# Loading a paged key/value cache: single pages from two queues, or gathers of 128 blocks from Pool

## The chip, the cores and the metric

The kernel runs on one core of a Trainium2 chip. The metric is the time of one execution on the device in microseconds. The engines have the names that the profile gives them: PE (TensorE, matmuls; PEld are its weight loads), DVE (VectorE), ACT (ScalarE), POOL (GpSimd) and SP (SyncE, which here only issues DMAs). SPq, POOLq and so on are the sequencers of these engines.

## What is computed

One step of a hybrid decoder layer: a prompt of 1024 tokens (causal attention over itself) and 8 sequences of 4 new tokens each, whose attention runs over 8192 cached tokens per sequence. The cache is paged. For the change only this part of the reference matters:

```python
k_past = cache_k[l, page_table].reshape(bs, past, N_HEADS, 2, QK_HEAD)
v_past = cache_v[l, page_table].reshape(bs, past, N_HEADS, V_HEAD)
k_all = jnp.concatenate([k_past.astype(k.dtype), k], axis=1)
v_all = jnp.concatenate([v_past.astype(v.dtype), v], axis=1)
o = diff_attend(q, q_pos_s, k_all, v_all, k_pos_s, lam)
```

`page_table` has 8 x 64 page numbers. A page holds 128 tokens; a token's keys (and its values) are 4 heads x 128 numbers of 4 bytes, so 2 KB, and a page is 256 KB of keys and 256 KB of values. All of it together is 512 pages x 2 x 256 KB, some 268 MB. Every cached token is visible to every query, so the order in which the tokens of a page lie in SBUF changes nothing, as long as keys and values have the same one.

## The kernel before, in words

The kernel has five stages, each closed by `stage_end`, where PE, ACT, DVE and SP wait for each other: (1) modulation, (2) the input projection, (3) attention, (4) output projection and the first half of the feed-forward, (5) the down projection. The change lies in stage 3, which in the trace runs from about 423 to 1287 us. The prompt's attention and the samples' attention are woven into each other there.

The samples are taken one after the other: `step(b, ...)` for b = 0 to 7. A step has REVS = 4 rounds r of RING = 4 groups g; a group is GP = 4 pages, so 1 MB of keys and 1 MB of values. `k_ring` and `v_ring` have four slots of one group each. In step b, for each group, DVE turns the keys (`turn_keys`, L1432, 32x32 blocks, `k_ring` to `k_turned`, and the slot is free when that is done: `k_free`), PE multiplies them with the queries (`key_group`, L852), and then PE multiplies the values of sample b-1 with the probabilities of sample b-1 (`value_group`, L862; the slot is free after it: `v_free`). So keys of b and values of b-1 are used side by side. In between lie the prompt's pieces (`scores` L818, `turn_rows` L825, `weigh_rows` L832, `maxima`, `combine`, `take_rows`): one tile of 128 prompt rows in each round, and the tiles differ in size (1, 2, 5, 6 or 0, 3, 4, 7 as multiples of 128 columns, plus one). Between two steps stands `softmax(b)`: scores of the sample to probabilities, turned by PE and copied to `p_t` (L424). It is a chain over PE, DVE and ACT in which no ring slot is used. After step 7 there are 16 value groups alone. PE and ACT run two steps in each turn of a loop, from step 1 on.

The pages are loaded by `load_pages` (L442 to L463), which runs on SP for the groups 0 and 2 and on Pool for the groups 1 and 3. For each page it reads the page's number from SBUF into a register (`value_load`), and before a group's first page it waits for the slot. Each page is a DMA of its own (L449) of 128 rows of 2 KB, token p to partition p. Its counts on `k_in[g]` and `v_in[g]` rise by 64 a group. In each queue the keys of b+1 and the values of b stand in turn. Pool issues one more transfer ahead of its pages: `v_rows` (L631, 2 MB, the prompt's values), after `conv_s_in`. DVE begins the stage with a memset (L1369) and a little work on `conv_s`. SP begins it with `page_row` (L552) and six small transfers.

Of the kernel before, what the change touches and what calls it, by code (L numbers as in the profile page):

```python
# [30 lines left out]
I32 = mybir.dt.int32  # L31
ALU = mybir.AluOpType
ACT = mybir.ActivationFunctionType
AX_X = mybir.AxisListType.X
ds = bass.ds

P = 128
QUAD = 32
# [31 lines left out]
def constants(z):  # L70

    p = np.arange(P)
    out = {}
    out["ident"] = np.eye(P)

    out["quad_fold"] = (p[:, None] % QUAD == np.arange(QUAD)[None, :])

    h, q = p // QUAD, p % 8
# [26 lines left out]
    where, n = {}, 0  # L105
# [6 lines left out]
def build(nc, z, io, const_at, n_const):  # L112
    T, D, B, S, H, HD, F = z.T, z.D, z.B, z.S, z.H, z.HD, z.F
    KC, NT, CH, NCH, NF, BS, AW, CC = z.KC, z.NT, z.CH, z.NCH, z.NF, z.BS, z.AW, z.CC
# [4 lines left out]
    GP, RING = 4, 4  # L119
    REVS = z.PAGES // (GP * RING)  # L120
    NEW0 = z.PAGES * QUAD
    SC = NEW0 + QUAD
# [5 lines left out]
    with ExitStack() as ctx:  # L128
# [27 lines left out]
        def sem(name):  # L156
            return ctx.enter_context(nc.semaphore(name))
# [56 lines left out]
        s_quads = ar("s_quads", [P, 2, WB])  # L214
        dense_end = max(ar.at, stage0 + 4 * ((2 * RING + 2) * GP * AW + B * z.PAGES + NT * AW + SC + 2 * T + P + 64))
        ar.at = dense_end
# [17 lines left out]
        ar.at += 2 * GP * AW * 4 - 7 * CC * 4  # L234
        page_row = ar("page_row", [1, B * z.PAGES], mybir.dt.int32)
        v_rows = ar("v_rows", [P, NT, AW])
# [56 lines left out]
        v_out = io["new_v_prompt"].rearrange("l b t h d -> (l b t) (h d)")  # L293
        k_pages = io["cache_k"].rearrange("l n p h d -> (l n) p (h d)")
        v_pages = io["cache_v"].rearrange("l n p h d -> (l n) p (h d)")
        x_dram = io["x_prompt"].rearrange("b t d -> (b t) d")
# [45 lines left out]
        v_in = [sem(f"v_in{g}") for g in range(RING)]  # L342
        pages_in = sem("pages_in")
        k_free, v_free, scored, s_bank_free = sem("k_free"), sem("v_free"), sem("scored"), sem("s_bank_free")
# [94 lines left out]

        def load_pages(eng, par):  # L440


            def group(pages, ring, landed, free, b, r, g):
                for j in range(GP):
                    page = eng.value_load(page_row[0:1, ds((b * REVS + r) * (RING * GP) + (g * GP + j), 1)],  # L445
                                          min_val=0, max_val=z.POOL - 1)
                    if j == 0:
                        eng.wait_ge(free, (b * REVS + r) * RING + g + 1)
                    eng.dma_start(ring[:, g, j, :], pages[ds(page, 1)].rearrange("o p d -> p (o d)")  # L449
                                  ).then_inc(landed[g], 16)  # L450

            keys, values = (k_pages, k_ring, k_in, k_free), (v_pages, v_ring, v_in, v_free)
            with eng.Fori(0, REVS) as r:
                for g in range(par, RING, 2):
                    group(*keys, 0, r, g)
            with eng.Fori(0, B - 1) as b:
                with eng.Fori(0, REVS) as r:
                    for g in range(par, RING, 2):
                        group(*keys, b + 1, r, g)
                        group(*values, b, r, g)  # L460
            with eng.Fori(0, REVS) as r:
                for g in range(par, RING, 2):
                    group(*values, B - 1, r, g)  # L463

# [6 lines left out]
        def _(sp):  # L471
# [79 lines left out]

            sp.dma_start(page_row[:], io["page_table"].rearrange("b n -> (b n)").rearrange("(o n) -> o n", o=1)).then_inc(pages_in, 16)  # L552
            for j in range(3):
                sp.dma_start(conv_s[:, j, :], u_ext[:, j:j + S, :]).then_inc(conv_s_in, 16)
            for j in range(3):
                sp.dma_start(conv_s[:, 4 + j, :], io["conv_w"][0, j].partition_broadcast(QUAD)).then_inc(conv_s_in, 16)
            sp.wait_ge(pages_in, 16)
            load_pages(sp, 0)
            stage_end(sp, 3)
# [68 lines left out]
        def _(pool):  # L628
# [3 lines left out]

            pool.wait_ge(pages_in, 16)
            load_pages(pool, 1)


# [27 lines left out]
        def _(pe):  # L664
# [192 lines left out]
            def value_group(b, r, g, stop):  # L857

                pe.wait_ge(v_in[g], (b * REVS + r + 1) * (16 * GP))
                for j in range(GP):  # L860
                    for h in range(H):
                        last = mm(psum[QUAD * h:QUAD * (h + 1), 2, 0:P], p_t[:, (r * RING + g) * GP + j, :],  # L862
                                  v_ring[:, g, j, h * HD:(h + 1) * HD], start=False, stop=stop and j == GP - 1)
                last.then_inc(v_free, 1)
# [362 lines left out]
        def _(dve):  # L1227
# [139 lines left out]
            dve.sem_inc(o_free, 1)  # L1367
            dve.sem_inc(scored, 2)
            link(v.memset(q_zero[:], 0.0))  # L1369
            dve.wait_ge(conv_s_in, 96)  # L1370
# [57 lines left out]
            def turn_keys(b, r, g):  # L1428
                n = (b * REVS + r) * RING + g
                dve.wait_ge(k_in[g], (b * REVS + r + 1) * (16 * GP))  # L1430
                dve.wait_ge(scored, n + 1)
                v.transpose(k_turned[:, g % 2].rearrange("p j n -> p (j n)"), k_ring[:, g].rearrange("p j n -> p (j n)")  # L1432
                            ).then_inc(k_free, 1)
# [267 lines left out]
```

## Time and profile before

| | us |
|---|---|
| median of 3 runs | 2371.07 (2368.57 to 2372.17) |
| the profiled execution, its own time | 2369.3 |
| its span in the trace | 2367.6 |
| granted clock of PE, mean share of 2.4 GHz | 0.88 |
| stage 3 in the trace | about 423 to 1287 |

The span is cut into 40 slices of 59.2 us in the page's second part; stage 3 fills about the 8th to the 22nd of them. A digit there is the busy share in tenths. A row of the timeline begins with start and duration in us; the square brackets at its end say how long the engine had been idle before it and what ended that. In the row of a window, "DMA share" is the mean busy share of the 16 DMA engines. It can be over 1, since the packets of an engine overlap.

### The profile page before, as it was taken

To read this page: it belongs to the slowest core of one execution; us is meant where nothing else is said; L and a number is where in the kernel's file an instruction comes from. 1 tells how busy PE (TensorE), PEld (TensorE's weight loads), DVE (VectorE), ACT (ScalarE), POOL (GpSimd) and SP (SyncE) were. 2 spreads that over 40 slices of the span, in tenths; PEclk is the share of its full clock that TensorE was granted. 3 is DMA by queue.
4 is the path that set the end of the run, shared out by engine and by line. 5 is a ranking of instruction groups with operands and counts; after the bars stand their busy time and mean duration, and the time that the engine had idled before them with its cause. 6 is when DMAs were issued, how large, how long until landed. Compare 5 with 4: busy or idle time off the path is not lost.

```text
span 2367.6 us, 47877 instructions
## 1 busy us (share of the span) xinstructions
PE 1879.2 (79%) x17492; PEld 1497.8 (63%) x17492; DVE 1058.0 (45%) x1528; ACT 488.9 (21%) x831; POOL 354.9 (15%) x544
## 2 busy tenths in 40 slices
PE   5699999567565765766665894999999997999992
PEld 1378899345444554544544893777777776888881
DVE  2424221666675675666661567121112112455457
ACT  0300111021212112121220204111211111333331
POOL 0000000223242432334332106100000000000003
PEclk7799999578887877878886897999999998999996
DMA  9611222789898989989888210121212123311112
GB/s 311 250 36 35 72 71 101 255 259 334 295 386 289 386 300 327 337 290 386 315 310 285 107 46 8 55 70 55 86 55 69 56 86 139 128 41 37 37 32 91
DMA packets 210968, 404.21 MB, mean 171 GB/s; under 512 B 24426, under 2 KB 88938, under 8 KB 210788
## 3 DMA queue, kind: packets, MB, share of 16 engines
q1 hardware_dynamic: 161012, 261.51, 31.9%
q0 software_dynamic: 41488, 136.35, 15.6%
q10 hardware_dynamic: 8320, 4.19, 0.6%
q8 instruction: 116, 1.90, 0.3%
q14 instruction: 32, 0.26, 0.0%
HBM read 377.53 MB, written 24.51 MB: 170 GB/s over the span
## 4 chain that ended last, share of the span: by engine, by line
PE 60%; SPq 13%; DVE 10%; DMA 9%; issue 6%; ACT 1%; DVEq 0%; ACTq 0%
PE psum L753 26%; PE psum L1002 11%; PE psum L761 10%; SPq L445 7%; SPq L449 6%; DMA v_ring<-cache_v 4%; DMA ada_w<-w_ada 3%; DVE k_turned L1432 2%; PE psum L1009 2%; DVE p_t L424 2%; PE psum L736 2%; PE psum L862 1%; DVE x_lo L1282 1%; DMA k_ring<-cache_k 1%; PE psum L852 1%
## 5 line engine op out<-in xcount | busy, mean ns | idle before, releaser
L1432 DVE STREAM_TRANSPOSE k_turned<-k_ring 128x2048 f32<-128x2048 f32 x128 | 295.4, 2308 | 12.6 <-DMA k_ring<-cache_k 12.3
L753 PE MATMUL psum<-x_hi,w_hi 128*128 128x512 f32 x896 | 281.3, 395 | 0.0
L852 PE MATMUL psum<-k_turned,q_blocks 128*32 128x128 f32 x4096 | 171.2, 319 | 136.2 <-DVE k_turned L1432 136.1
L753 PE MATMUL psum<-x_lo,w_hi 128*128 128x512 f32 x896 | 277.2, 391 | 0.0
L753 PE MATMUL psum<-x_hi,w_lo 128*128 128x512 f32 x896 | 276.1, 389 | 0.0
L852 PEld LDWEIGHTS psum<-k_turned,q_blocks 128*32 128x32 f32 x4096 | 127.9, 128 | 194.8 <-issue 148.2
L1301 DVE TENSOR_TENSOR w_lo<-w_raw,w_hi 128x2048 fp32r<-128x2048 f32 x37 | 86.9, 2350 | 361.9 <-ACT w_hi L1057 352.2
L862 PE MATMUL psum<-v_ring,p_t 128*32 128x128 f32 x4096 | 173.9, 325 | 65.1 <-DMA v_ring<-cache_v 65.0
L1002 PE MATMUL psum<-d_hi,h_hi 128*128 128x256 f32 x704 | 209.2, 297 | 12.1 <-DVE d_lo L1646 11.0
L1002 PE MATMUL psum<-d_lo,h_hi 128*128 128x256 f32 x704 | 199.9, 284 | 0.0
L1002 PE MATMUL psum<-d_hi,h_lo 128*128 128x256 f32 x704 | 199.7, 284 | 0.0
L753 PEld LDWEIGHTS psum<-x_hi,w_hi 128*128 128x128 f32 x896 | 165.7, 188 | 44.9 <-ACT h_out L1193 4.5
L449 POOL DMA_DIRECT2D k_ring<-cache_k x256 | 139.0, 543 | 363.5 <-issue 182.4
L862 PEld LDWEIGHTS psum<-v_ring,p_t 128*32 128x32 f32 x4096 | 140.0, 132 | 83.5 <-DMA v_ring<-cache_v 79.1
L753 PEld LDWEIGHTS psum<-x_lo,w_hi 128*128 128x128 f32 x896 | 168.8, 188 | 35.7
L753 PEld LDWEIGHTS psum<-x_hi,w_lo 128*128 128x128 f32 x896 | 168.5, 188 | 35.9
L761 PE MATMUL psum<-w_hi,x_hi 128*128 128x256 f32 x640 | 182.9, 286 | 0.0
L761 PE MATMUL psum<-w_lo,x_hi 128*128 128x256 f32 x640 | 181.8, 284 | 0.0
L761 PE MATMUL psum<-w_hi,x_lo 128*128 128x256 f32 x640 | 181.8, 284 | 0.0
L1645 DVE TENSOR_TENSOR h_lo<-h_all,h_hi 128x1024 fp32r<-128x1024 f32 x88 | 107.6, 1223 | 145.6 <-ACT d_hi L1218 145.6
L449 POOL DMA_DIRECT2D v_ring<-cache_v x256 | 138.5, 541 | 208.5 <-issue 175.2
L1002 PEld LDWEIGHTS psum<-d_hi,h_hi 128*128 128x128 f32 x704 | 135.1, 192 | 48.1 <-issue 44.4
(228 smaller groups left out, 2562.0 us busy)
## 6 DMA issues: line engine op xcount, KB each, us to landing
k_ring<-cache_k SPq DMA_DIRECT2D x256, 256.0 KB, 8.1
k_ring<-cache_k POOLq DMA_DIRECT2D x256, 256.0 KB, 6.1
v_ring<-cache_v SPq DMA_DIRECT2D x256, 256.0 KB, 8.9
v_ring<-cache_v POOLq DMA_DIRECT2D x256, 256.0 KB, 6.1
ada_w<-w_ada SPq DMA_DIRECT2D x12, 2048.0 KB, 9.2
w_raw<-w_in SPq DMA_DIRECT2D x12, 1024.0 KB, 5.2
w_raw<-w_gate SPq DMA_DIRECT2D x11, 1024.0 KB, 5.3
w_raw<-w_up SPq DMA_DIRECT2D x11, 1024.0 KB, 6.2
```

The source lines that it names most:

```text
L424: last = copy(to[QUAD * a:QUAD * (a + 1), :, j], got[:, :, :, a, :])
L445: page = eng.value_load(page_row[0:1, ds((b * REVS + r) * (RING * GP) + (g * GP + j), 1)], min_val=0, max_val=z.POOL - 1)
L449: eng.dma_start(ring[:, g, j, :], pages[ds(page, 1)].rearrange("o p d -> p (o d)")).then_inc(landed[g], 16)
L736: last = mm(psum[q:q + QUAD, 4 + s, 0:WB], x_t_s[:, k, :], w_raw[:, s, k, :], start=k < 4, stop=k >= KC - 4)
L753: last = mm(psum[:, 2 * ft + c, 0:CH], w[:, s, k, ft * P:(ft + 1) * P], x[:, k, c * CH:(c + 1) * CH], start=k == 0 and j == 0, stop=k == K ...
L761: last = mm(psum[:, t % TB, 0:WB], x[:, k, t * P:(t + 1) * P], w[:, s, k, :], start=k == 0 and j == 0, stop=k == KC - 1 and j == 2)
L852: last = mm(psum[QUAD * h:QUAD * (h + 1), g % 2, 0:GP * QUAD], q_blocks[:, h, d, :], k_turned[:, g % 2, :, h * HD + d * QUAD:h * HD + (d + ...
L862: last = mm(psum[QUAD * h:QUAD * (h + 1), 2, 0:P], p_t[:, (r * RING + g) * GP + j, :], v_ring[:, g, j, h * HD:(h + 1) * HD], start=False, ...
L1002: last = mm(psum[:, down_bank(par, pair), (t % 2) * WB:(t % 2 + 1) * WB], x[:, s, t * P:(t + 1) * P], w[:, s, :], start=k == 0 and j == 0 ...
L1301: v.tensor_tensor(w_lo[:, s], w_raw[:, s], w_hi[:, s], ALU.subtract).then_inc(w_lo_done, 1)
L1432: v.transpose(k_turned[:, g % 2].rearrange("p j n -> p (j n)"), k_ring[:, g].rearrange("p j n -> p (j n)")).then_inc(k_free, 1)
L1645: v.tensor_tensor(h_lo[:, s, :], h_all[:, k, :], h_hi[:, s, :], ALU.subtract)
```

## The change

The pages come in gathers. A page is seen as 32 blocks of 8 KB (four tokens each), and one indirect DMA brings 128 blocks, which is a group of four pages: partition 32 j + a gets block a of the group's page j. The numbers of the blocks stand in `page_idx`, one column for each group. DVE makes it in four instructions, one for each j, from `page_all`, which is the page table spread over all partitions: 32 x page + lane, where lane is a new constant. All gathers, 128 of keys and 128 of values, are issued by Pool, written out without loops and without register loads; SP issues no pages any more. Each group now counts 16 on its semaphore. What PE, ACT and DVE do with the rings stays the same.

```diff
+    out["lane"] = (p % QUAD)[:, None]
...
-        page_row = ar("page_row", [1, B * z.PAGES], mybir.dt.int32)
+        page_all = ar("page_all", [P, B * z.PAGES], I32)
+        page_idx = ar("page_idx", [P, B * z.PAGES // GP], mybir.dt.uint32)
...
-        k_pages = io["cache_k"].rearrange("l n p h d -> (l n) p (h d)")
-        v_pages = io["cache_v"].rearrange("l n p h d -> (l n) p (h d)")
+        k_pages = io["cache_k"].rearrange("l n (p s) h d -> (l n p) (s h d)", p=QUAD)
+        v_pages = io["cache_v"].rearrange("l n (p s) h d -> (l n p) (s h d)", p=QUAD)
...
-        def load_pages(eng, par):
...
+        def load_pages(pool):
+            def gather(rows, ring, landed, free, b, r, g):
+                n = (b * REVS + r) * RING + g
+                pool.wait_ge(free, n + 1)
+                pool.indirect_dma_start(ring[:, g].rearrange("p s d -> p (s d)"), None, rows,
+                                        bass.IndirectOffsetOnAxis(page_idx[:, n:n + 1], 0)).then_inc(landed[g], 16)
+            for b in range(B + 1):
+                for r in range(REVS):
+                    for g in range(RING):
+                        if b < B:
+                            gather(k_pages, k_ring, k_in, k_free, b, r, g)
+                        if b:
+                            gather(v_pages, v_ring, v_in, v_free, b - 1, r, g)
...
-            sp.dma_start(page_row[:], io["page_table"].rearrange("b n -> (b n)").rearrange("(o n) -> o n", o=1)).then_inc(pages_in, 16)
+            sp.dma_start(page_all[:], io["page_table"].rearrange("b n -> (b n)").partition_broadcast(P)).then_inc(pages_in, 16)
...
-            sp.wait_ge(pages_in, 16)
-            load_pages(sp, 0)
             stage_end(sp, 3)
...
-            pool.wait_ge(pages_in, 16)
-            load_pages(pool, 1)
+            pool.wait_ge(page_idx_ready, GP)
+            load_pages(pool)
...
-                pe.wait_ge(v_in[g], (b * REVS + r + 1) * (16 * GP))
+                pe.wait_ge(v_in[g], (b * REVS + r + 1) * 16)
...
+            dve.wait_ge(pages_in, 16)
+            for j in range(GP):
+                r = slice(QUAD * j, QUAD * (j + 1))
+                v.tensor_scalar(page_idx[r, :], page_all[r, :].rearrange("p (n j) -> p n j", j=GP)[:, :, j], float(QUAD), C("lane")[r],
+                                ALU.mult, ALU.add).then_inc(page_idx_ready, 1)
             link(v.memset(q_zero[:], 0.0))
...
-                dve.wait_ge(k_in[g], (b * REVS + r + 1) * (16 * GP))
+                dve.wait_ge(k_in[g], (b * REVS + r + 1) * 16)
```

## Rows read from the trace of the kernel before

**Rows 1.** The page's second part: busy tenths and GB/s in 40 slices.
```profile
DVE  2424221666675675666661567121112112455457
DMA  9611222789898989989888210121212123311112
GB/s 311 250 36 35 72 71 101 255 259 334 295 386 289 386 300 327 337 290 386 315 310 285 107 46 8 55 70 55 86 55 69 56 86 139 128 41 37 37 32 91
```
**Rows 2.** The page's fourth part: the chain that ended last, by engine.
```profile
PE 60%; SPq 13%; DVE 10%; DMA 9%; issue 6%; ACT 1%; DVEq 0%; ACTq 0%
```
**Rows 3.** Windows: stretch, length, busy us of each engine, PE clock, DMA share, GB/s.
```profile
742.00:750.00 8.00, 6.89 (x130) 5.35 (x130) 6.00 (x9) 1.47 (x6) 1.62 (x3) 0.63 0.56 171
760.00:830.00 70.00, 50.65 (x863) 38.44 (x864) 43.58 (x56) 14.03 (x38) 28.89 (x53) 0.83 1.04 386
834.00:844.00 10.00, 2.04 (x42) 1.25 (x42) 8.62 (x21) 2.02 (x4) 0.00 (x0) 0.50 0.08 31
1250.00:1284.00 34.00, 18.91 (x352) 14.25 (x352) 0.00 (x0) 0.00 (x0) 11.65 (x22) 0.65 0.98 349
```
**Rows 4.** Timeline of DVE: first or last keys turned, steps 0, 1, 3, 4, 6, 7.
```profile
442.05 2.31 DVE L1432 STREAM_TRANSPOSE k_turned<-k_ring 128x2048 f32<-128x2048 f32 x1 [0.62 <-DMA k_ring<-cache_k]
511.58 2.30 DVE L1432 STREAM_TRANSPOSE k_turned<-k_ring 128x2048 f32<-128x2048 f32 x1
534.28 2.31 DVE L1432 STREAM_TRANSPOSE k_turned<-k_ring 128x2048 f32<-128x2048 f32 x1
740.30 2.31 DVE L1432 STREAM_TRANSPOSE k_turned<-k_ring 128x2048 f32<-128x2048 f32 x1
813.75 2.30 DVE L1432 STREAM_TRANSPOSE k_turned<-k_ring 128x2048 f32<-128x2048 f32 x1
841.96 2.31 DVE L1432 STREAM_TRANSPOSE k_turned<-k_ring 128x2048 f32<-128x2048 f32 x1
1126.26 2.30 DVE L1432 STREAM_TRANSPOSE k_turned<-k_ring 128x2048 f32<-128x2048 f32 x1
1149.01 2.30 DVE L1432 STREAM_TRANSPOSE k_turned<-k_ring 128x2048 f32<-128x2048 f32 x1
```
**Rows 5.** Waits: engine and line, what for, us in total, times, longest.
```profile
PEld psum L862 <- DMA v_ring<-cache_v: 79.1, 45, 6.3
PE psum L862 <- DMA v_ring<-cache_v: 65.0, 40, 6.0
```
**Rows 6.** Timeline: page issues of SP (four in a row) and of Pool.
```profile
742.79 3.83 SPq L449 DMA_DIRECT2D k_ring<-cache_k  x4
747.65 4.68 SPq L449 DMA_DIRECT2D v_ring<-cache_v  x4
818.28 3.85 SPq L449 DMA_DIRECT2D v_ring<-cache_v  x4
...
746.36 0.54 POOL L449 DMA_DIRECT2D k_ring<-cache_k  x1 [21.92 <-DVE k_turned L1432]
747.59 0.54 POOL L449 DMA_DIRECT2D k_ring<-cache_k  x1 [0.69 <-issue]
```
**Rows 7.** Timeline: Pool's 2 MB issue, and one page issue beside DVE's L1393.
```profile
429.73 1.07 POOL L631 DMA_DIRECT2D v_rows<-new_v_prompt  x1 [429.12 <-DMA conv_s<-conv_w]
...
811.91 0.86 POOL L449 DMA_DIRECT2D k_ring<-cache_k  x1 [0.69 <-issue]
811.96 0.69 DVE L1393 TENSOR_SCALAR a_rows<-e_rows,soft 128x896 f32<-128x896 f32 x1
```
**Rows 8.** Timeline and window in stage 4: a 4 MB load in rows of 4 KB.
```profile
1312.22 0.37 SPq L566 DMA_DIRECT2D x<-x_prompt  x1
...
1316.00:1324.00 8.00, 8.00 (x54) 6.78 (x55) 0.00 (x0) 0.00 (x0) 0.00 (x0) 0.66 1.02 415
```
**Rows 9.** Timeline of PE: first and last value groups after step 7.
```profile
1243.26 5.18 PE L862 MATMUL psum<-v_ring,p_t 128*32 128x128 f32 x128
...
1282.38 3.73 PE L862 MATMUL psum<-v_ring,p_t 128*32 128x128 f32 x64 [1.60 <-DMA v_ring<-cache_v]
```
**Rows 10.** Timeline: SP's table load and DVE's work at the start of stage 3.
```profile
423.73 0.25 SPq L552 DMA_DIRECT2D page_row<-page_table  x1
...
425.14 1.76 DVE L1369 MEMSET q_zero<- 128x2048 f32 x1 [9.18 <-issue]
429.17 2.11 DVE L1372 TENSOR_TENSOR conv_s<-conv_s 32x512 f32<-32x512 f32 x3 [2.26 <-DMA conv_s<-conv_w]
```

More of the change, by code:

```diff
@@ L214, in build @@
         s_quads = ar("s_quads", [P, 2, WB])
-        dense_end = max(ar.at, stage0 + 4 * ((2 * RING + 2) * GP * AW + B * z.PAGES + NT * AW + SC + 2 * T + P + 64))
+        dense_end = max(ar.at, stage0 + 4 * ((2 * RING + 2) * GP * AW + B * z.PAGES + B * z.PAGES // GP + NT * AW + SC + 2 * T + P + 64))
         ar.at = dense_end
@@ L342, in build @@
         v_in = [sem(f"v_in{g}") for g in range(RING)]
-        pages_in = sem("pages_in")
+        pages_in, page_idx_ready = sem("pages_in"), sem("page_idx_ready")
         k_free, v_free, scored, s_bank_free = sem("k_free"), sem("v_free"), sem("scored"), sem("s_bank_free")
@@ L437, in build @@
         block = ctx.enter_context(nc.Block())
-        def load_pages(eng, par):
[L443 to L463, printed above, removed]
+        def load_pages(pool):
[11 more added lines that the diff above has]
+                            gather(v_pages, v_ring, v_in, v_free, b - 1, r, g)
         def fetch_head(eng, h):
```

## The prediction

> **What bounds the kernel now.** I looked first at the slices of the page. Stage 3, some 864 of 2368 us, is the only long stretch in which the DMA engines stand at 8 or 9 tenths, while DVE stands at 5 to 7 there [rows 1]. The chain that ended last gives 60% to PE (mostly the projections outside stage 3), and 22% to SP's sequencer and DMA together [rows 2], and these two are what the change touches. The windows say what that is: inside a step the DMA engines are full, share 1.04, and move 386 GB/s, while PE is busy 50.65 and DVE 43.58 of 70 us [rows 3]. Between two steps they stand nearly still, 31 GB/s, since all eight ring slots are full and the softmax chain uses none. So a step is paced partly by the transfer, and the softmax between steps by its own chain. That consumption waits for data is seen in the waits: PE's value groups waited 79.1 us (weight loads) and 65.0 us (matmuls) for `v_ring`; the two overlap, so it is some 80 us, not 144 [rows 5].
>
> The period of a step is (1149.01 - 534.28) / 6 = 102.5 us [rows 4]. It moves 32 groups of 1.049 MB, 33.6 MB, which at 386 GB/s is 86.9 us. Some 15 us of DMA time per step are lost, partly in the stand-still, partly in the ramp after it: in the first 8 us of a step the engines moved only 171 GB/s [rows 3], because SP needs 4.9 us to issue the four pages of a group (742.79 to 747.65) and Pool 1.22 us for each page (746.36 to 747.59) [rows 6].
>
> **Part 1: who issues, and at what cost.** Now SP and Pool each issue half. SP needs 75.5 us for 15 groups (742.79 to 818.28), 5.0 us each, without a stop for a slot [rows 6]. Both together can thus issue a group in about 2.5 us, and the DMA engines take 1.049 / 0.386 = 2.72 us for it. After the change Pool alone must issue one gather per group. If it costs less than about 2.5 us, it is hidden behind the transfer; if it costs more, Pool becomes the bound. No row shows an indirect DMA. The near rows: Pool's issue of 128 rows of 2 KB is 0.54 us [rows 6], and that of 1024 such rows is 1.07 us [rows 7], so rows cost Pool almost nothing in a plain issue (0.53 us for 896 more). From below, then, a gather costs 0.54 us. From above I take a gather as four page issues with their register loads, 4 x 1.22 = 4.9 us, as if each quarter's table had to be read by itself. The value I take is 1.2 to 2 us, near one page issue with one look into SBUF, because the instruction names 128 blocks and no page issue's fixed part should be paid four times. It is hidden. Both ends stay in the rivals.
>
> Break-even. If Pool stands still for the 28 us between steps (813.75 to 841.96 is 28.2 us, 1126.26 to 1149.01 is 22.7 us, from the last keys turned to the first [rows 4]) it must issue 24 gathers in the rest: (102.5 - 28 - 5) / 24 = 2.9 us. If it uses that time for the eight refills, 102.5 / 32 = 3.2 us. Above about 3 us per gather the kernel gets slower.
>
> **Part 2: the transfer.** Pages come in rows of 2 KB now, blocks of 8 KB later. Nothing here moves 8 KB rows, but a load in rows of 4 KB ran at 415 GB/s over 8 us with a DMA share of 1.02 [rows 8], against 386 for the pages [rows 3]. So a group takes between 2.72 us (nothing gained) and 2.53 us (415 GB/s); I take 2.55. Below 386 I see no reason from rows, except for a gather that is spread unevenly over the 16 engines; that goes with the slow rival. Over the 24 groups that must arrive inside a step this is 65.2 us before and 61.2 after, 4 us less per step.
>
> **Part 3: order and ramp.** SP and Pool drift apart: by 818.28 SP has issued its last group of the step's cycle [rows 6] while Pool still lags some 7 us, so keys of the next sample go ahead of values that PE waits for now. One queue keeps the order of use. Also the first free slot is refilled by one instruction and not over 4.9 us. Both take the ramp of about 5 us and part of the V waits away. The floor is then the consumption by itself: step 0, without any value stream, needs 511.58 - 442.05 = 69.5 us from the first to the last keys turned, about 3 of it waits for the first loads, and step 3 needs 73.5 us [rows 4]. The mean over the steps 1 to 7 (112 such transposes, of which the first and last of step 3 stand there) is 74.4. I take 70 for each: 4.4 x 7 = 31 us. The bound from the other side is the same pace as now, 0, and at best 66, which is 59 us. The stretch between two steps is 102.5 - 74.4 = 28 us on average and 22.7 at its shortest (after step 6), and a part of the difference is the last value group landing late. Another part is the turning point of PE's loop and the head's work, and stays. Of 6 x 5.4 = 32 us I take 10.
>
> **Part 4: the end.** After step 7 sixteen value groups run alone. The first four come from full slots (1243.26), the last ends at 1286.1 [rows 9]. Twelve groups took from 1244.6 (the first of the four done) to 1286.1, 3.46 us each, at 349 GB/s with the DMA share below 1 [rows 3], since a slot is refilled page by page, four times 1.22 us. A single gather needs its issue and the transfer, 12 x 2.6 to 2.9 + 3 for the first landing: 34 to 38 us instead of 41.5. I take 6 us less.
>
> **Part 5: the start.** DVE now waits for the table before its memset and has four small instructions more (32 partitions x 128 numbers, about 0.3 us each by the L1372 rows' 0.7 us for 512). The table was issued at 423.73 and the memset began at 425.14; after it DVE stood idle 2.26 us [rows 10]. So 2 to 3 us more meet 2.3 us of cover: 0 to 1 us. SP's table load is 256 KB now and not 2 KB, ahead of the six small ones, less than 1 us at 386 GB/s. Pool's wait for `page_idx` stands behind `conv_s_in`, which comes later (429.73 [rows 7]); behind it are all gathers, and DVE's first keys wait for them. Before, SP began pages beside Pool's `v_rows`; now 2 MB of `v_rows` stand ahead of the first keys in the one queue. Step 0 waited for its keys 0.62 us at 442.05 [rows 4]; 3.1 MB at 386 GB/s are 8.1 us from 431, about 440. I take 0, with 3 us either way. SP is free and only reaches the stage's end earlier: nothing. That keys and values of one queue wait for each other in turn (behind a wait for `v_free` stand the next keys) costs nothing as long as the ring is four deep: the order of waiting is that of use.
>
> **Sum.** 31 + 10 + 6 + 0 = 47 us off the profiled execution's 2369.3 us, 2322. It lay 1.8 us below the median of the runs, so 2324 us. The ends of the terms: 0 + 0 + 3 - 3 = 0 us with nothing hidden gained, and 59 + 20 + 8 + 3 = 90 us at best, 2281.
>
> **A rule against it.** One page issue beside DVE's L1393 took Pool 0.86 us and not 0.54 [rows 7]. The Trainium skill (SBUF — State Buffer, "SBUF: two separate sides") says that a DMA issued from GpSimd can't get its descriptors written while DVE runs an operation in a two-port mode, and that DMAs from SP are free of this; the change moves half of the pages from SP to Pool. That row would agree, with 0.3 us.
>
> **The rivals.** (A) Pool is the bound: a gather costs more than about 3 us because each of the 128 block numbers is worked on by itself. For it: no row shows one, and the plain rows cover a regular pattern only. Against it: 1024 rows in 1.07 us. At 3.5 us the period is 32 x 3.5 = 112 us, 9.5 more, 67 for seven steps and 1 at the end: 2371 + 68 = 2439 us. At 4.9 us it is 157 us, and some 2770. It decides from 3.0 us on. (B) The pages land sooner, but nobody needs them sooner: DVE and PE pace the step as they do in step 0 with its small waits. Then only the end and a third of Part 3 remain, 6 + 12 = 18 us: 2353. For it speaks the irregular pace of the transposes with the ring full. (C) Pool's issues are held up by DVE. At most the time of L1393, 0.69 us in the row, in each of the 28 rounds of seven steps falls on the path: 19 us of the 47 are lost, 2343. (D) The gathers gain what the lost second queue costs (two queues side by side kept each DMA engine fed): about 2371.
>
> **How the numbers follow.** Forecast, 2285 to 2340: 0.50. (A) slower, from about 2376 up: 0.24, half of it above 2430. (B) and (C), 2340 to 2366: 0.17. (D), within 0.2%, 2366 to 2376: 0.08. Better than 2285: 0.01. A difference of 0.2%, 4.7 us, is about what a measurement of this kernel can tell from none. Faster 0.68, same 0.08, slower 0.24. The range of 8 in 10 goes from 2288 to 2430 and leaves out about 0.02 below and 0.12 to 0.15 above. The likeliest case's own range is 2285 to 2340.
>
> **What would show it.** In the profile after: gathers on Pool with a mean duration below 2.5 us, and Pool idle before them mostly for `k_turned` or `v_ring`; in a step's middle 400 GB/s and more; the DMA slices of stage 3 no higher than now, but fewer; PE's waits for `v_ring` far below 79.1 us; the period of a step near 96 us; the value groups at the end 3 us apart. The prediction is wrong if Pool is back to back in its gathers and the GB/s of a step's middle fall below 386, which is (A), or if the waits for `v_ring` vanish and the period stays above 100 us, which is (B).

## The result, and the profile after

The changed kernel takes 2299.79 us in the median of 4 runs (2296.46 to 2304.27), the kernel before 2370.01 us beside it. The ratio is 0.9704 (95% interval 0.9685 to 0.9723): 70 us or 3.0% faster, where 2324 us was predicted, in a range of 2288 to 2430. The profiled execution took 2304.27 us, 65.0 us less than the profiled one of before.

The page of the changed kernel: the DMA engines and the chain.

```profile
DVE  2324121577776685776734564111121112465547
DMA  9701132677898988989975110121212214311102
GB/s 312 265 30 43 37 109 92 232 288 300 334 410 321 418 330 327 414 330 396 363 311 224 37 37 19 55 91 55 73 55 69 77 55 173 106 42 38 37 28 94
...
PE 65%; DVE 17%; DMA 11%; issue 5%; ACT 1%; DVEq 0%; POOL 0%; SPq 0%; ACTq 0%
...
L448 POOL DMA_INDIRECT k_ring<-cache_k,page_idx x128 | 120.6, 943 | 330.8 <-DVE k_turned L1429 322.0
L448 POOL DMA_INDIRECT v_ring<-cache_v,page_idx x128 | 120.7, 943 | 207.3 <-PE psum L854 199.9
```

A gather costs Pool 0.943 us, and Pool is idle before it because a ring slot is not free yet (322.0 and 199.9 us of waiting). SP's sequencer, 13% of the chain before [rows 2], is gone from it, and DVE rose from 10 to 17%. Slices of stage 3 now reach 418 GB/s where they reached 389 [rows 1].

Windows in the middle of steps 1, 3 and 4 of the changed kernel (columns as in rows 3), and the waits of PE and its weight loads for `v_ring`:

```profile
560.00:580.00 20.00, 13.60 (x311) 10.28 (x299) 16.52 (x19) 4.49 (x11) 8.43 (x9) 1.00 1.01 417
740.00:760.00 20.00, 13.47 (x336) 10.43 (x336) 16.32 (x22) 3.94 (x12) 8.55 (x10) 1.00 1.01 418
840.00:860.00 20.00, 15.09 (x304) 12.01 (x308) 15.79 (x22) 3.32 (x9) 8.02 (x9) 0.89 1.01 419
...
PEld psum L854 <- DMA v_ring<-cache_v,page_idx: 17.7, 12, 3.1
PE psum L854 <- DMA v_ring<-cache_v,page_idx: 13.3, 12, 2.8
```

The rate rose from 386 [rows 3] to 417 to 419 GB/s with the engines full in both cases, and the waits for values fell from 79.1 and 65.0 us [rows 5] to 17.7 and 13.3. The twelve that are left are those after step 7. The first and last keys turned of steps 0, 1, 3, 4 and 7:

```profile
443.95 2.30 DVE L1429 STREAM_TRANSPOSE k_turned<-k_ring 128x2048 f32<-128x2048 f32 x1
507.67 2.30 DVE L1429 STREAM_TRANSPOSE k_turned<-k_ring 128x2048 f32<-128x2048 f32 x1
531.70 2.31 DVE L1429 STREAM_TRANSPOSE k_turned<-k_ring 128x2048 f32<-128x2048 f32 x1
721.16 2.31 DVE L1429 STREAM_TRANSPOSE k_turned<-k_ring 128x2048 f32<-128x2048 f32 x1
788.18 2.31 DVE L1429 STREAM_TRANSPOSE k_turned<-k_ring 128x2048 f32<-128x2048 f32 x1 [0.47 <-DMA k_ring<-cache_k,page_idx]
814.36 2.31 DVE L1429 STREAM_TRANSPOSE k_turned<-k_ring 128x2048 f32<-128x2048 f32 x1
1094.07 2.30 DVE L1429 STREAM_TRANSPOSE k_turned<-k_ring 128x2048 f32<-128x2048 f32 x1
```

Step 3 went from 73.5 us [rows 4] to 67.0, the period of a step from 102.5 to (1094.07 - 531.70) / 6 = 93.7. Taken over all steps (128 transposes in each trace), the 65 us are made up like this, in us:

| part of stage 3 | before | after | difference |
|---|---|---|---|
| up to the first keys turned (442.05, 443.95) | | | +1.9 |
| step 0, first to last keys turned | 69.5 | 63.7 | -5.8 |
| steps 1 to 7, mean | 74.3 | 67.1 | 7 x -7.25 = -50.8 |
| between steps 0 and 1 | 22.7 | 24.0 | +1.3 |
| between the others, mean | 28.0 | 26.7 | 6 x -1.28 = -7.7 |
| last keys turned to the last value group's end | 63.4 | 59.5 | -3.9 |
| sum | | | -65.0 |

Behind the last value group 1081.5 us of the span were left before and 1081.3 are now. All of the gain lies in stage 3, and four fifths of it inside the steps with both streams. Only that line of the table is steady. A second profiled execution of the changed kernel (the run `after_again` below) has 67.1 us for the steps 1 to 7 too, but 66.8 for step 0, 26.1 for the mean stretch between steps and 61.6 for the end.

In the steps 1 to 7 of before PE waited 48.3 us for values (32 times) and DVE 9.6 us for keys (11 times). In the changed kernel there is no such wait for values, and 5.1 us for keys are left. That is 52.8 us less, about the 50.8 of the table. The clock of PE moved as well. The sums of the seven steps, from the first to the last keys turned, before and after:

```profile
sum 520.40, PE 356.56 PEld 262.45 DVE 367.75 ACT 82.50 POOL 198.31; mean PE 50.94 PEld 37.49 DVE 52.54 ACT 11.79 POOL 28.33
sum 469.64, PE 331.93 PEld 252.92 DVE 367.87 ACT 82.65 POOL 187.83; mean PE 47.42 PEld 36.13 DVE 52.55 ACT 11.81 POOL 26.83
```

DVE is busy for as long as before, PE for 3.5 us less a step, at a granted clock of 0.82 to 0.87 before and 0.88 to 0.94 after (1.0 is 2.4 GHz, 0.5 is 1.2 GHz). How much of the gain comes through the clock, and whether it rose because PE waited less, no run separates.

### The profile page after: what moved, and what is told of

Same layout as the page of the kernel before. It is cut to its first block, busy times and chain, and to the rows that moved or that the text cites. A ratio compares the mean times of both kernels' runs of the same rounds, so it can differ in the third digit from the quotient of the medians.

```text
span 2302.5 us, 40476 instructions
## 1 busy us (share of the span) xinstructions
PE 1839.8 (80%) x17492; PEld 1481.2 (64%) x17492; DVE 1056.6 (46%) x1532; ACT 489.0 (21%) x831; POOL 319.1 (14%) x287
## 4 chain that ended last, share of the span: by engine, by line
PE 65%; DVE 17%; DMA 11%; issue 5%; ACT 1%; DVEq 0%; POOL 0%; SPq 0%; ACTq 0%
PE psum L745 27%; PE psum L994 12%; PE psum L753 10%; DVE k_turned L1429 6%; DMA k_ring<-cache_k,page_idx 6%; DMA ada_w<-w_ada 3%; PE psum L844 2%; PE psum L854 2%; PE psum L1001 2%; DVE p_t L426 2%; PE psum L728 2%; PE psum L824 1%; DVE x_lo L1274 1%; DMA v_ring<-cache_v,page_idx 1%; DVE soft L1380 1%
## 5 line engine op out<-in xcount | busy, mean ns | idle before, releaser
L844 PE MATMUL psum<-k_turned,q_blocks 128*32 128x128 f32 x4096 | 157.0, 300 | 151.0 <-DVE k_turned L1429 150.7
L844 PEld LDWEIGHTS psum<-k_turned,q_blocks 128*32 128x32 f32 x4096 | 117.0, 119 | 204.6 <-issue 152.9
L854 PE MATMUL psum<-v_ring,p_t 128*32 128x128 f32 x4096 | 163.9, 307 | 17.6 <-DMA v_ring<-cache_v,page_idx 13.3
L448 POOL DMA_INDIRECT k_ring<-cache_k,page_idx x128 | 120.6, 943 | 330.8 <-DVE k_turned L1429 322.0
L994 PEld LDWEIGHTS psum<-d_hi,h_hi 128*128 128x128 f32 x704 | 135.0, 192 | 48.3 <-issue 44.1
L854 PEld LDWEIGHTS psum<-v_ring,p_t 128*32 128x32 f32 x4096 | 136.4, 125 | 25.3 <-DMA v_ring<-cache_v,page_idx 17.7
L448 POOL DMA_INDIRECT v_ring<-cache_v,page_idx x128 | 120.7, 943 | 207.3 <-PE psum L854 199.9
```

The lines of the kernel that those rows point to most:

```text
L448: pool.indirect_dma_start(ring[:, g].rearrange("p s d -> p (s d)"), None, rows, bass.IndirectOffsetOnAxis(page_idx[:, n:n + 1], 0)).then_i ...
L844: last = mm(psum[QUAD * h:QUAD * (h + 1), g % 2, 0:GP * QUAD], q_blocks[:, h, d, :], k_turned[:, g % 2, :, h * HD + d * QUAD:h * HD + (d + ...
L994: last = mm(psum[:, down_bank(par, pair), (t % 2) * WB:(t % 2 + 1) * WB], x[:, s, t * P:(t + 1) * P], w[:, s, :], start=k == 0 and j == 0 ...
```

## The experiments

Three causes were in question, all of them touched by the change: the size of the rows in which pages come (2 or 8 KB), the order in which two queues or one bring the groups, and the price of the issue (eight register loads and DMAs for a pair of groups, or two instructions). The kernel before was timed beside each of them, and ratios (with their 95% interval) are against it. Not all kernels ran on the same chip, so the ratio is the better measure where two of them are compared. The diffs show the line that matters; the views of the cache, counts and waits that change with it are left out.

**Plain DMAs of 1 MB from Pool.** In `load_pages` of the changed kernel:

```diff
-                pool.indirect_dma_start(ring[:, g].rearrange("p s d -> p (s d)"), None, rows,
-                                        bass.IndirectOffsetOnAxis(page_idx[:, n:n + 1], 0)).then_inc(landed[g], 16)
+                pool.dma_start(ring[:, g], rows[n * GP:(n + 1) * GP].rearrange("j p d -> p j d")).then_inc(landed[g], 16)
```

> The changed kernel, but each gather is a plain DMA from Pool of four neighbouring pages (1 MB), in rows of 2 KB, token p of each page to partition p. It leaves the page table out of account: pages are read in their order in the pool. One queue, one instruction a group and the order of use are as in the changed kernel; only the rows are those of before. Theory R (the gain is the rate of 8 KB blocks against 2 KB rows): the middle of a step stays at 386 GB/s, the steps from first to last keys turned stay at 71 to 74 us, time 2340 to 2365 us. Theory I (the gain is one cheap issue in the order of use, and the row size is no matter): 2295 to 2310 us with steps of 67 us.

2337.15 us, ratio 0.9863 (0.9841 to 0.9885). That is in the range of neither theory, 3 us below that of R. Theory R was right on what it said of the rate, 384 GB/s, and of the steps:

```profile
560.00:580.00 20.00, 12.30 (x278) 9.23 (x282) 14.66 (x20) 3.43 (x9) 6.02 (x8) 1.00 1.02 384
```

The steps 1 to 7 take 71.1 us on average, and late in a step keys are turned 5.4 us apart with a wait for `k_ring` before them (the last two of step 3 stand here). That is two groups at 386 GB/s, 2 x 2.72, so here the transfer sets the pace:

```profile
797.81 2.31 DVE L1428 STREAM_TRANSPOSE k_turned<-k_ring 128x2048 f32<-128x2048 f32 x1 [0.79 <-DMA k_ring<-cache_k]
803.23 2.31 DVE L1428 STREAM_TRANSPOSE k_turned<-k_ring 128x2048 f32<-128x2048 f32 x1 [0.89 <-DMA k_ring<-cache_k]
```

But the time is 31 us below before with the same rows and the same rate. So not quite half of the gain had to be looked for in the issue or the order.

**The same in blocks of 8 KB, from Pool.**

```diff
+                pool.dma_start(ring[:, g].rearrange("p s d -> p (s d)"), rows[n * P:(n + 1) * P]).then_inc(landed[g], 16)
```

> As the kernel with plain DMAs of 1 MB from Pool, but in blocks of 8 KB, 128 neighbouring blocks to the 128 partitions. It leaves the page table out of account too. Against the changed kernel only the indirection is gone. Both theories: 2295 to 2305 us, as the changed kernel, 415 to 420 GB/s in the middle of a step; the issue on Pool 0.5 us and not 0.94. If the gather's own cost or its spread over the DMA engines matters, this one is faster by more than 5 us.

2296.22 us, ratio 0.9691 (0.9672 to 0.9710), 417 to 418 GB/s, steps of 66.4 us, with 0.55 us for an issue on Pool where the gather takes 0.943. It is 41 us faster than its twin with 2 KB rows on the same chip. The indirection of the real kernel costs nothing that these runs can tell: 0.9704 and, in a later comparison, 0.9689.

**Both from SP.** The call of `load_pages` moves from Pool to SP, behind the wait for the table; nothing else.

> The plain DMAs of 1 MB in rows of 2 KB, issued by SP and not by Pool (the page table is left out of account, as there). Theory R: as from Pool, 2340 to 2365 us, 377 to 390 GB/s. Theory I: 2295 to 2310 us. If DMAs from Pool suffer from DVE, this one is faster than its twin from Pool by more than 5 us.

> The plain DMAs of 1 MB in blocks of 8 KB, issued by SP (the page table is left out of account). Both theories: 2295 to 2305 us. If DMAs from Pool suffer from DVE: 2285 to 2295 us.

2328.11 us (0.9827, 0.9809 to 0.9845) with 2 KB and 2293.48 us (0.9681, 0.9664 to 0.9698) with 8 KB. Against Pool they are 9 and 3 us faster. The first pair's intervals only just touch, the second's overlap. The 9 us are more than the 5 us that the expectation named as the sign of DVE holding up Pool's DMAs. But Pool's issues of the values have 751 ns as shortest and as median and 760 as longest, so DVE did not hold those issues up. In windows of 20 us the 2 KB kernel from SP shows 376 to 385 GB/s and that from Pool 361 to 384; inside the steps both reach 386. Of the 9 us 4.5 lie in the steps 1 to 7 (70.4 us each and not 71.1). What they are stays open.

**Smaller blocks, more gathers.** The table gets two or four columns for a group, and `gather` issues as many instructions, each of 128 blocks of 4 KB or of 2 KB:

```diff
+                for m in range(2):
+                    pool.indirect_dma_start(ring[:, g, 2 * m:2 * (m + 1)].rearrange("p s d -> p (s d)"), None, rows,
+                                            bass.IndirectOffsetOnAxis(page_idx[:, 2 * n + m:2 * n + m + 1], 0)).then_inc(landed[g], 16)
```

> The changed kernel with two gathers a group, each of 128 blocks of 4 KB (two pages), and a table twice as wide, made by two DVE instructions. A gather takes Pool 0.94 us, with 0.30 us between two in a row: 2.5 us a group, just under the transfer's 2.5 to 2.6 us. Rival A of the prediction puts the break-even near 3 us a group: so still faster than before, 2300 to 2325 us. The rate in the middle of a step is 400 to 415 GB/s, by the 4 KB load in stage 4.

> The changed kernel with four gathers a group, each of one page in 128 rows of 2 KB. Pool needs 4 x 1.24 = 5.0 us a group: Pool is the bound. By rival A's formula the period of a step is 32 x 5.0 = 159 us, 65 more than in the changed kernel, times seven, and the steps 0 and 8 move 16 groups each at 5.0 us: 2300 + 457 + 40 = about 2800 us. If a gather's cost goes with its bytes and not with its blocks, it is far less, below 2400 us.

Two gathers: 2316.98 us, ratio 0.9782 (0.9763 to 0.9801), steps of 68.9 us. Four: 2812.68 us (a single execution), within 13 us of what rival A's formula gave. Both windows, first of two and then of four gathers a group, and Pool in the latter:

```profile
740.00:760.00 20.00, 13.12 (x282) 10.05 (x285) 15.81 (x21) 2.69 (x9) 15.12 (x17) 0.91 1.03 409
```
```profile
740.00:760.00 20.00, 11.11 (x141) 8.57 (x142) 6.27 (x7) 1.11 (x3) 15.13 (x17) 0.50 0.70 210
...
763.63 0.95 POOL L448 DMA_INDIRECT k_ring<-cache_k,page_idx  x1 [0.30 <-issue]
764.88 0.95 POOL L448 DMA_INDIRECT k_ring<-cache_k,page_idx  x1 [0.30 <-issue]
```

Pool is back to back at 1.25 us a gather, 5.0 us a group, and 1.049 MB / 5.0 us are the 210 GB/s. A gather's price does not go with its bytes. All gathers here have 128 block numbers, so no run tells a price for each number from a price for the instruction. With two, Pool needs 2.5 us a group and the transfer 2.56 at 409 GB/s; that is below the break-even of about 3 us and still faster than before. It also gives the third point for the rate: rows of 2 KB 384 to 386, blocks of 4 KB 407 to 409, of 8 KB 415 to 420 GB/s, with the DMA engines full each time.

**Blocks of 8 KB in the kernel before.** Page j of a group goes to the partitions 32 j to 32 j + 31, everything else as before:

```diff
-                    eng.dma_start(ring[:, g, j, :], pages[ds(page, 1)].rearrange("o p d -> p (o d)")
+                    eng.dma_start(ring[QUAD * j:QUAD * (j + 1), g].rearrange("p s d -> p (s d)"), pages[ds(page, 1)].rearrange("o p d -> p (o d)")
```

> The kernel before (SP and Pool, one DMA for each page with register loads), but a page goes as 32 blocks of 8 KB to 32 partitions and not as 128 rows of 2 KB to 128 partitions. Theory R: some of the gain comes although the issue stays as it was, 2325 to 2345 us. Theory I: 2360 to 2375 us. A third possibility is that 32 partitions are served by fewer DMA engines at a time, and the kernel gets slower than 2371 us.

2703.86 us (five executions, 2670.54 to 2716.00), ratio 1.1443 (1.1411 to 1.1474): neither of the two theories, but the third possibility, as far as the direction goes. The engines are not fewer, however:

```profile
740.00:760.00 20.00, 9.76 (x171) 7.52 (x160) 6.32 (x6) 1.22 (x3) 4.49 (x9) 0.68 1.02 238
```

The share is 1.02, so the engines are full on average, and they move 238 GB/s (220 to 273 in other stretches of the stage). The Trainium skill (SBUF — State Buffer, "Door 1: The DMA port swizzle") says that 32 neighbouring partitions, and also the first 64, reach only eight of SBUF's sixteen ports for DMA. That fits this row; no run here tells it from another limit on 32 partitions. The size of the DMA is not what makes it slow, since before moved the same 256 KB at a time over 128 partitions at 386 GB/s. Of the forms tried here, the gather alone brings scattered pages in blocks of 8 KB over all 128 partitions.

**Order or price of the issue.** The plain DMAs of 1 MB in 2 KB rows, but SP issues the groups 0 and 2 and Pool 1 and 3 (`for g in range(par, RING, 2)`), as in the kernel before:

> The plain DMAs of 1 MB in rows of 2 KB (page table left out of account), but issued as before by two queues: SP the groups 0 and 2, Pool 1 and 3. Against the kernels with one queue only the order across the queues is as before; against the kernel before only the issue is cheap (one instruction a group, no register loads). Part 3 of the prediction put the drift of the two queues against each other beside the slow issue as a cause. If the drift counts: 2345 to 2365 us. If only the price and delay of the issue count: 2325 to 2340 us, as with one queue.

2372.31 us, ratio 0.9998 (0.9983 to 1.0013), 7 us above the range for the drift. That is the time of the kernel before, although each group costs one instruction and no register load. Against one queue from Pool the second queue costs 35 us, or 32 by the ratios. The rate is the same; this window and these rows are of step 3:

```profile
760.00:820.00 60.00, 38.44 (x758) 28.26 (x758) 41.36 (x49) 10.35 (x26) 7.48 (x10) 0.86 1.03 386
...
PEld psum L855 <- DMA v_ring<-cache_v: 67.9, 30, 4.8
...
754.15 0.37 SPq L448 DMA_DIRECT2D v_ring<-cache_v  x1
...
773.49 1.93 PE L855 MATMUL psum<-v_ring,p_t 128*32 128x128 f32 x31 [3.98 <-DMA v_ring<-cache_v]
```

SP's issue at 754.15 is the sixth group of the step (743.87, 747.23, 747.67, 751.28 and 752.03 come before it in the two queues). Six groups at 386 GB/s are 16.3 us, so in the order of issue it would have been there about 762. By the trace it landed 19.3 us after its issue, at 773.4, and PE waited 3.98 us for it. Pool's issue of 757.84, made later, took 12.6 us and had landed at 770.4. With two queues later groups move at the same time as the one that is needed first, and can land before it. The queues do not share the engines evenly either. The view of the DMA queues from 760 to 780 us (packets, MB, share of the engines; then issues with the us from issue to landing):

```profile
q0 software_dynamic: 1275, 4.95, 64.3%
q1 hardware_dynamic: 1377, 2.73, 37.8%
...
v_ring<-cache_v SPq DMA_DIRECT2D x2, 1024.0 KB, 21.5
v_ring<-cache_v POOLq DMA_DIRECT2D x2, 1024.0 KB, 10.4
```

q0 is Pool's queue and q1 is SP's. Both move about as many packets, but Pool's hold 3.9 KB on average and SP's 2.0, so SP's groups take twice as long to land. In the kernel with one queue PE's waits of the steps are gone: 20.3 us in 12 waits are left, the twelve after step 7. DVE's waits for keys rose in turn, from 13.4 us (15 times) to 34.6 (39 times).

The equal times of this kernel and of before do not show that the price of the issue is worth nothing. The parts differ: step 0 takes 63.3 us here and not 69.5, and the steps 1 to 7 take 75.7 and not 74.3. In before Pool needs 1.22 us for each page, and its queue and SP's move about the same there, 13.70 and 13.18 MB from 760 to 830 us. The cheap issue lifted that limit, and Pool's queue went ahead of SP's. What the issue alone is worth in two queues with 2 KB rows stays open.

**Two queues with 8 KB.**

> The plain DMAs of 1 MB in blocks of 8 KB (page table left out of account), issued by two queues, SP the groups 0 and 2, Pool 1 and 3. With rows of 2 KB the second queue cost 35 us (2372 against 2337). If queue and block size are independent causes: 2296 + 35, so 2325 to 2335 us, with the steps near 71 us and 415 GB/s. If the faster blocks make the order of landing harmless, since the transfer no longer paces the step: 2295 to 2310 us.

2300.64 us, ratio 0.9713 (0.9688 to 0.9737), steps of 66.4 us:

```profile
740.00:760.00 20.00, 13.85 (x338) 10.73 (x337) 16.39 (x21) 4.27 (x12) 2.65 (x5) 1.00 1.01 416
...
PEld psum L855 <- DMA v_ring<-cache_v: 27.0, 20, 5.5
```

The causes don't add up: with 8 KB blocks the second queue costs nothing that can be told from the one-queue ratio of 0.9691. The view of the queues (760 to 780 us) shows one difference, beside the higher rate:

```profile
q0 software_dynamic: 570, 4.16, 50.8%
q1 hardware_dynamic: 568, 4.15, 50.0%
...
v_ring<-cache_v SPq DMA_DIRECT2D x2, 1024.0 KB, 18.3
v_ring<-cache_v POOLq DMA_DIRECT2D x2, 1024.0 KB, 18.1
```

Both queues have packets of 7.3 KB on average (small ones counted in) and move the same, and their groups land after the same time. Which of the two, the even share or the transfer that no longer sets the pace, makes the second queue harmless, no run separates.

| plain DMAs of 1 MB | rows of 2 KB | blocks of 8 KB |
|---|---|---|
| two queues | 0.9998 | 0.9713 |
| one queue (Pool) | 0.9863 | 0.9691 |

Alone, the block size brings 2.9% and the single queue 1.4% (1.7% when SP issues it); together they bring 3.1%.

**A version that is faster.** From step 7 on the key ring has nothing to hold, and the twelve waits that are left are for values. The last sample's groups 4 to 7 and 12 to 15 are loaded into `k_ring` (and read there by `value_group`), and DVE's memset stands ahead of its wait for the table. In the first form the eight gathers of the groups 8 to 15 went alternately to `k_ring` and `v_ring`, in the second the four for `v_ring` go first:

```diff
+                        if b == B:
+                            last = RING + (B - 1) * REVS * RING + g + 1
+                            if r == 0:
+                                gather(v_pages, k_ring, k_in, k_free, B - 1, 1, g, RING + (B * REVS - 1) * RING + g + 1)
+                                gather(v_pages, v_ring, v_in, v_free, B - 1, 0, g, last - RING)
+                            elif r == 2:
+                                gather(v_pages, v_ring, v_in, v_free, B - 1, 2, g, last)
+                            elif r == 3:
+                                gather(v_pages, k_ring, k_in, v_free, B - 1, 3, g, last + RING)
+                            continue
```

> The changed kernel with two edits: the values of the last sample also go into the key ring, which is free then (second and fourth round), so that four more groups are there when the last softmax ends; and the memset of q_zero stands ahead of DVE's wait for the table. The first takes 4 x 2.5 = 10 us from the end of the stage, the second 1 to 2 us from its start: 2286 to 2290 us. If the DMA engines are not idle after step 7, or the start waits for the keys anyway: 2295 us.

> The version with the last sample's values in both rings, with the order of the last eight gathers put right: the four that go into the value ring come first, as they are used first and their slots are free first (from about 1180 us on and not from 1185). The eight need 20 us and 3 for the landing: the last value group ends near 1206 us and not at 1215.9, so 2281 to 2286 us, and 14 us or more below the changed kernel beside it. If the order was not the fault of its forerunner: 2292 us again.

> The changed kernel once more, as the measure for its neighbours on the same chip: 2297 to 2303 us.

The first form took 2292.61 us (0.9675, 0.9657 to 0.9693), while 2286 to 2290 was expected; its rows show why. PE waits 7.16 us for the first of the eight and then about 3 us each for the next ones used, because each stands behind one that is used four groups later:

```profile
1194.83 1.94 PE L864 MATMUL psum<-v_ring,p_t 128*32 128x128 f32 x32 [7.16 <-DMA v_ring<-cache_v,page_idx]
```

The second took 2285.96 us (0.9639, 0.9614 to 0.9663), the changed kernel beside it 2301.86 (0.9689, 0.9664 to 0.9714): 16 us less by the medians, 12 by the ratios, where 14 or more was expected, and the two intervals just miss each other at 0.9663 and 0.9664. In the two profiled executions the last value group ends 13.0 us earlier (1208.97, not 1221.97; expected was 1206). Another 5.6 us lie behind it, where the two kernels are the same, and are no gain of the edit. The last value group now begins here:

```profile
1207.03 1.94 PE L867 MATMUL psum<-k_ring,p_t 128*32 128x128 f32 x32 [1.39 <-DMA k_ring<-cache_v,page_idx]
```

Eight waits for values of at most 2.2 us are left. It beats both kernels. What the moved memset brings is small: from SP's load of the table to the first keys turned it is 18.1 us in the first form and 18.7 in the second, and 18.9 and 19.2 in the two executions of the changed kernel.

## Why the prediction was right, and where it was not

**Direction and mechanism** held: gathers hidden under the transfer, a higher rate, fewer waits for values. The time was 24 us below the forecast, inside the range and near its lower edge, because the largest term of the sum was too small.

**Part 1, the issue.** Taken as 1.2 to 2 us a gather, measured 0.943 and 1.24 from start to start in a row. Rival A fell for this kernel, and its formula stood in the kernel with four gathers: 2800 us expected for 5.0 us a group, 2812.7 measured. Of the two bounds the low one, Pool's plain issue of 0.54 us, was the nearer. The gather was cheaper than the value taken.

**Part 2, the rate.** 415 GB/s from the load in rows of 4 KB was near enough: 417 to 419. (Gathers of 4 KB blocks ran at 407 to 409, so the nearness is partly luck.) What the rate is worth was not read rightly. It was reckoned as 4 us less transfer per step and has no term of its own in the sum, where consumption was to cap the gain at 70 us a step. The runs make the block size the strongest single cause (0.9998 to 0.9713 with two queues).

**Part 3, order and ramp.** The term that was mis-sized: 31 us for the steps, 50.8 measured. The failed step is the floor, read as "the consumption by itself" from step 0 with its 69.5 us. The windows of step 0 show what it was: before, the changed kernel, and the second profiled execution of the changed kernel.

```profile
442.05:511.58 69.53, 45.21 (x534) 28.77 (x534) 52.38 (x64) 11.70 (x34) 16.91 (x31) 0.67 0.83 264
443.95:507.67 63.72, 37.96 (x534) 25.09 (x534) 52.24 (x65) 11.78 (x34) 16.68 (x18) 0.79 0.79 292
443.00:509.82 66.82, 42.01 (x534) 27.26 (x534) 52.28 (x65) 11.68 (x34) 16.73 (x18) 0.70 0.75 281
```

The work is the same, 534 matmul records each time, and DVE is as busy in all three. But PE took 45.21 us for it at a mean clock of 0.67, 42.01 at 0.70 and 37.96 at 0.79. In before 2.1 of the 69.5 us are waits for keys inside the step (1.20 and 0.94 us; the prediction had named some 3 and taken 70 nevertheless). They are gone in the changed kernel. The rest of the difference goes along with the time that PE spent at the lower of its two clock levels, and why that time differs from one execution to the next stays open. So 69.5 us were no floor. The steps 1 to 7, with both streams and a clock of 0.82 to 0.87, had a floor at or below the 67.1 us that they came to, near the best bound of 66. Of the two reasons given, the drift of the queues has its support in 2 KB rows with one instruction a group (32 to 35 us). The slow refill by single issues is not shown to have cost anything: the first 8 us of step 3 moved 171 GB/s before, 216 in two queues with one instruction a group and 201 in the changed kernel, and the kernel with 216 was the slowest of the three; but it differs from before in more than the refill. Between the steps 7.7 - 1.3 = 6.4 us went, for 10 taken (9.9 in the second profiled execution).

**Part 4, the end.** 3.9 us for 6 taken (1.8 in the second profiled execution). PE's value groups after step 7 of the changed kernel, the first four, the fifth and sixth, and the last two:

```profile
1182.01 5.89 PE L854 MATMUL psum<-v_ring,p_t 128*32 128x128 f32 x128
1189.78 1.08 PE L854 MATMUL psum<-v_ring,p_t 128*32 128x128 f32 x32 [1.88 <-DMA v_ring<-cache_v,page_idx]
1193.68 1.93 PE L854 MATMUL psum<-v_ring,p_t 128*32 128x128 f32 x32 [2.82 <-DMA v_ring<-cache_v,page_idx]
...
1217.12 1.93 PE L854 MATMUL psum<-v_ring,p_t 128*32 128x128 f32 x32 [0.39 <-DMA v_ring<-cache_v,page_idx]
1219.60 1.56 PE L854 MATMUL psum<-v_ring,p_t 128*32 128x128 f32 x32 [0.55 <-DMA v_ring<-cache_v,page_idx]
```

The last groups come 2.3 and 2.5 us apart, a little less than the 2.6 to 2.9 reckoned, and twelve groups took 37.2 us from the end of the first of the four, inside the 34 to 38. The first two of them show waits of 1.88 and 2.82 us. A group is used only when it has landed whole, and its slot and the next load wait for that.

**Part 5, the start.** 1.9 us later for 0, with 3 us allowed either way; 1.3 of them lie ahead of stage 3 already (SP's table load at 425.04, not 423.73 as in rows 10). DVE waited for the table, as its rows show, and the memset ahead of which it waited comes 4.8 us later than in rows 10. Most of that is covered again: from SP's table load to the first keys turned it is only 0.6 us more than before, and 0.9 in the second profiled execution:

```profile
428.09 1.39 DVE L1364 TENSOR_SCALAR page_idx<-page_all,consts 32x128 uint32<-32x128 int32 x4 [10.82 <-DMA page_all<-page_table]
429.97 1.76 DVE L1366 MEMSET q_zero<- 128x2048 f32 x1 [0.49 <-issue]
```

**The rivals.** (B) was wrong as a time, 2353 us, and right as a mechanism to come next: in the 8 KB kernels the steps stand at 66 to 67 us with one queue or two and with or without the indirection, with next to no waits for data (5.1 us for keys in seven steps of the changed kernel). (C) is not seen: the value gathers' shortest is 932 ns and their median 936 (the longest 1707), and the mean over all 256 gathers, 943 ns, is 11 ns above the shortest, 2.8 us in all. So what the Trainium skill (SBUF — State Buffer, "SBUF: two separate sides") says about DMAs from GpSimd beside DVE cost at most that in issue time here. The 9 us between Pool and SP with 2 KB rows are not explained by it and stay open. (D) had it the wrong way round: the second queue did not feed the engines better, both layouts show a share of 1.01 to 1.04.

**The signs.** Gathers under 2.5 us, 400 GB/s and more, few waits for `v_ring` and a period near 96 us (93.7) came as said. The slices of stage 3 reach more GB/s than before, where no more was expected, and the value groups at the end are 2.5 us apart and not 3.

## What to carry to other kernels

When the DMA engines are full, ask first how long the contiguous rows are and over how many partitions a transfer goes. In this kernel the price of the gathers was hidden until Pool was back to back. A stream that is used in a fixed order is safer in one queue, issued in that order, as long as the transfer paces it, since a second queue lets later pieces move at the same time as the one that is needed first. And a floor taken from a stretch of the same kernel is only a floor if its own waits are taken out first and its granted clock is that of the stretch it stands for.

## What was not expected of the hardware

Rows of 2 KB, blocks of 4 KB and of 8 KB ran at 386, 409 and 418 GB/s with equally full DMA engines, so a busy share of 1 does not mean the same rate. Blocks of 8 KB over 32 partitions at a time ran at 238 GB/s with a share of 1.02. Two queues that both carried 2 KB rows did not share the engines evenly: Pool's moved 4.95 MB and SP's 2.73 in the same 20 us. And a gather of 128 blocks cost Pool 0.94 us whether a block had 2, 4 or 8 KB.
